# Expert layer: gate and up sums of the two-block items taken with the weights standing still and 192 rows moving

## The reference, cut to what matters

```
def expert_block(args):
    tok, e = args
    xb = u[tok]
    gu = xb @ w_gu[e] + b_gu[e]
    gate = jnp.minimum(gu[:, :D_FF], SWIGLU_LIMIT)
    up = jnp.clip(gu[:, D_FF:], -SWIGLU_LIMIT, SWIGLU_LIMIT)
    act = (up + 1) * gate * jax.nn.sigmoid(SWIGLU_ALPHA * gate)
    return act @ w_down[e] + b_down[e]
```

## Time and profile before

| | |
|---|---|
| median of 3 runs | 2235.86 us (2235.25 to 2238.87) |
| the profiled execution: its own time | 2238.45 us |
| the profiled execution: span in the trace | 2236.4 us |
| instructions in it | 34316 |
| PE busy | 2161.3 us, 97% of the span |
| DVE busy | 1698.4 us, 76% |
| ACT busy | 1364.3 us, 61% |
| DMA | 548.15 MB, 245 GB/s in the mean |
| granted TensorE clock | 0.98 of full speed in the mean |

### The profile page before, as it was taken

The page is one execution under the profiler, slowest core; times in us unless marked ns, Lnnn a source line. Parts: engine busy times, 40 slices in busy tenths (PEclk is TensorE's granted clock), DMA queues, the critical chain, the costliest instruction groups (busy, mean ns, idle before and its releaser), DMA issues. The chain is left out here.

```text
span 2236.4 us, 34316 instructions
## 1 busy us (share of the span) xinstructions
PE 2161.3 (97%) x10582; PEld 1773.3 (79%) x10583; DVE 1698.4 (76%) x2091; ACT 1364.3 (61%) x1632; POOL 396.6 (18%) x436
## 2 busy tenths in 40 slices
PE   7999999979959999999999999999999999999997
PEld 7987777757848888888888888888888888888884
DVE  5426667776667668879979978679996669997897
ACT  4324665543446556757757756568775557776775
POOL 0000000003331221312212212212220122221121
PEclk9999999989969999999999999999999999999997
DMA  4111101227868667969969969669996669998897
GB/s 163 41 47 34 57 34 43 100 64 208 211 206 294 233 227 281 365 244 367 371 242 367 368 240 332 239 239 383 373 380 242 218 235 334 392 364 316 295 366 288
DMA packets 106509, 548.15 MB, mean 245 GB/s; under 512 B 17911, under 2 KB 28664, under 8 KB 51546
## 3 DMA queue, kind: packets, MB, share of 16 engines
q1 hardware_dynamic: 87850, 504.63, 60.7%
q0 software_dynamic: 18608, 42.85, 8.0%
HBM read 516.18 MB, written 41.47 MB: 249 GB/s over the span
## 5 line engine op out<-in xcount | busy, mean ns | idle before, releaser
L2343 DVE TENSOR_TENSOR wl<-raw,wh 128x2048 fp32r<-128x2048 f32 x423 | 958.5, 2285 | 43.1 <-PE sums L2165 26.8
L2227 ACT ACTIVATE wh<-raw 128x2048 fp32r<-128x2048 f32 x425 | 806.0, 1915 | 92.5 <-DMA raw<-in_w_experts 50.2
L2149 PE MATMUL sums<-wh,xh 128*128 128x512 f32 x1120 | 438.0, 391 | 0.0
L2148 PE MATMUL sums<-wl,xh 128*128 128x512 f32 x1120 | 438.0, 391 | 0.0
L2147 PE MATMUL sums<-wh,xl 128*128 128x512 f32 x1120 | 437.3, 390 | 0.0
L2082 POOL DMA_INDIRECT h_dram<-y,pairs_mine x47 | 121.4, 2584 | 808.9 <-DVE y L2396 485.0
L2148 PEld LDWEIGHTS sums<-wl,xh 128*128 128x128 f32 x1120 | 210.8, 188 | 45.1
L2149 PEld LDWEIGHTS sums<-wh,xh 128*128 128x128 f32 x1120 | 210.8, 188 | 44.7
L2147 PEld LDWEIGHTS sums<-wh,xl 128*128 128x128 f32 x1120 | 211.2, 189 | 43.1
L2147 PE MATMUL sums<-wh,al 128*128 128x512 f32 x560 | 230.2, 411 | 0.6 <-DVE al L2387 0.2
L2149 PE MATMUL sums<-wh,ah 128*128 128x512 f32 x560 | 219.4, 392 | 0.0
(11 more groups left out here) (370 smaller groups left out, 3596.4 us busy)
## 6 DMA issues: line engine op xcount, KB each, us to landing
raw<-in_w_experts SPq DMA_DIRECT2D x426, 1024.0 KB
raw<-in_w_chan SPq DMA_DIRECT2D x20, 512.0 KB, 3.3
o_gate<-in_x SPq DMA_DIRECT2D x8, 512.0 KB, 5.5
raw<-in_w_out SPq DMA_DIRECT2D x8, 512.0 KB, 5.4
ht<-in_x SPq DMA_DIRECT2D x8, 512.0 KB, 8.1
h_dram<-ht SPq DMA_DIRECT2D x8, 512.0 KB
u_dram<-ut SPq DMA_DIRECT2D x8, 512.0 KB
h_all<-h_dram SPq DMA_DIRECT2D x8, 512.0 KB, 7.0
```

The lines of the kernel that those rows point to most:

```text
L2148: pe.matmul(out, hi[:, n, :], w_lo[:, kk, :], start=False, stop=False)
L2149: last = pe.matmul(out, hi[:, n, :], w_hi[:, kk, :], start=False, stop=half == 1 and kk == 3)
L2227: nc.scalar.activation(wh[ch % HIGHS][:, :, :], raw[ch % RAW][:, :, :], ACT.Copy).then_inc(h_split.sem, 1)
L2343: dve.tensor_tensor(wl[ch % LOWS][:, :, :], raw[ch % RAW][:, :, :], wh[ch % HIGHS][:, :, :], ALU.subtract).then_inc(l_split.sem, 1)
```

## The change

Two-block items alone compute the gate and up sums in another way. The weights stand still, in pieces of 128 inputs by 128 features, and all 192 tokens move. A new tile xx holds for each slice of inputs high x of the 192 rows and the rest of x of the 192 rows. For each of the 4 slices and 4 pieces of 128 features in a chunk (`by_weights`) one matmul moves 384 rows (high w by high x and rest of x) and one moves 192 (rest of w by high x). The sums have features on the partitions, so nothing is transposed for the down products, and there are no bias matmuls: ACT copies the 192 sums of rest of x (`copy_low`), DVE adds them and the bias, which is now a column (`fold`, own_bias), and clamps (`clamp_tiles`). Three pairs of PSUM banks (`ring`) take the sums in turn, and PE waits in `tile_free` and `begin_sums` until a pair is read. The second block's rows are transposed, and split by `high_second` and `low_second`, in two halves of 4 slices; chunk 0 waits for the first half, chunk 1 for the second. One chunk's `high` and one chunk's `low` move from the end of an item to the start of the next. `out` uses tile tg in place of hh. One table more (b_columns, 256 KB) and a table cut in two are loaded ahead of the expert layer. One-block items keep their products.

```diff
 HALF_ROWS = P // 2
+ROWS = P + HALF_ROWS
...
+            sp.dma_start(k.b_columns[:, :, :], k.d["b_columns"]).then_inc(small_loaded.sem, 16)
+            sp.dma_start(k.pick_cons[:, :], k.d["pick_consts"]).then_inc(small_loaded.sem, 16)
...
+        xx = sb("xx", [P, KT, 2, 2 * P], F32R)
+        xh, xl = xx[:, :, 0, 0:P], xx[:, :, 1, 0:P]
         ah, al = sb("ah", [P, KT, P], F32R), sb("al", [P, KT, P], F32R)
-
-        xb = sb("xb", [P, KT, P], F32R)
         ab = sb("ab", [P, KT, P], F32R)
-        sel = sb("sel", [P, 2, P], F32R)
-
-        tg = sb("tg", [P, 2, 256])
-        uc = sb("uc", [P, 2, 256])
-        hh = sb("hh", [H, 512])
-        av = [sb(f"av{s}", [P, 2, 256]) for s in range(2)]
+        sel = sb("sel", [P, P], F32R)
+        own_bias = sb("own_bias", [P, 4 * 4])
...
+        a_ps = ps("a_ps", [P, 2, 512])
+
+
+        ring = [k.sums[:, 0:2, :], k.sums[:, 2:4, :], a_ps[:, :, :]]
...
+            def begin_sums(i, g, blocks):
                 if g < 2:
                     pe.wait_ge(y_read.sem, y_read.at(i, g - 1))
+                elif blocks == 2 and g == 4:
+                    pe.wait_ge(gate_ready.sem, gate_ready.at(i, 4))
                 else:
                     pe.wait_ge(gu_read.sem, gu_read.at(i, g - 1))
 
-                for b in range(blocks if g < 4 else 0):
-                    pe.matmul(acc[g % 2][b][:, :], sel[:, b, :], bias[:, g * 512:(g + 1) * 512], start=True, stop=False)
+                if g < 4:
+                    pe.matmul(acc[g % 2][0][:, :], sel[:, :], bias[:, g * 512:(g + 1) * 512], start=True, stop=False)
+
+            def tile_free(i, g, j):
+
+                if g == 0:
+                    pe.wait_ge(y_read.sem, y_read.at(i, j // 2 - 1))
+                elif (g, j // 2) in ((1, 1), (2, 1), (3, 1)):
+                    pe.wait_ge(gate_ready.sem, gate_ready.at(i, g))
+                elif g > 1:
+                    pe.wait_ge(gu_read.sem, gu_read.at(i, g - 1))
+
+            def by_weights(i, ch):
+
+                g, half = GROUP_OF[ch], HALF_OF[ch]
+                pe.wait_ge(*low_done(i, ch))
+                w_hi, w_lo = wh[ch % HIGHS], wl[ch % LOWS]
+                for j in range(4):
+                    if half == 0 and j % 2 == 0:
+                        tile_free(i, g, j)
+                    out = ring[(2 * g + j // 2) % len(ring)][:, j % 2, :]
+                    own = slice(j * P, (j + 1) * P)
+                    for kk in range(4):
+                        n = half * 4 + kk
+                        pe.matmul(out[:, 0:2 * ROWS].rearrange("p (a b) -> p a b", b=ROWS), w_hi[:, kk, own], xx[:, n, :, 0:ROWS],
+                                  start=n == 0, stop=False)
+                        last = pe.matmul(out[:, 0:ROWS], w_lo[:, kk, own], xx[:, n, 0, 0:ROWS], start=False, stop=n == KT - 1)
+                    if half == 1 and j == 1:
+                        last.then_inc(gates_made.sem, 1)
+                last.then_inc(parts_used.sem, 1)
...
                 if blocks == 2:
                     pe.wait_ge(xg_loaded[1].sem, xg_loaded[1].at(i, 16))
-                    turn(1)
+                    for half in range(2):
+                        turn(1, range(4 * half, 4 * half + 4))
+                    for ch in range(8):
+                        if ch < 2:
+                            pe.wait_ge(x_low.sem, x_low.at(i, ch + 1))
+                        by_weights(i, ch)
                 else:
-                    pe.sem_inc(x_turned.sem, 1)
-                pe.wait_ge(sel_ready.sem, sel_ready.at(i, 1))
-                if blocks == 2:
-
-                    biases(i, 0, blocks)
-                    for ch in range(2):
-                        first_block(i, ch)
-                    pe.wait_ge(x_low.sem, x_low.at(i, 1))
-                    for ch in range(2):
-                        second_block(ch).then_inc(parts_used.sem, 1)
-                for ch in range(2 if blocks == 2 else 0, 8):
-                    products(i, ch, blocks)
-                    if ch >= 3 and ch % 2 == 1:
-                        turn_act(i, (ch - 3) // 2, blocks)
+                    pe.sem_inc(x_turned.sem, 2)
+                    pe.sem_inc(gates_made.sem, gates_made.per)
+                    pe.wait_ge(sel_ready.sem, sel_ready.at(i, 1))
+                    for ch in range(8):
+                        products(i, ch, blocks)
+                        if ch >= 3 and ch % 2 == 1:
+                            turn_act(i, (ch - 3) // 2)
...
+            def high_second(i, half):
+                act.wait_ge(x_turned.sem, x_turned.at(i, half + 1))
+                at = slice(4 * half, 4 * half + 4)
+                nc.scalar.activation(xx[:, at, 0, P:ROWS], x_ps[:, at, 0:H], ACT.Copy).then_inc(x_high.sem, 1)
+
+            def copy_low(i, g, part):
+
+                if g == 0 and part == 0:
                     act.wait_ge(y_read.sem, y_read.at(i, 0))
+                if part == 0:
+                    act.wait_ge(gates_made.sem, gates_made.at(i, g + 1))
+                    to = tg[:, 0:2 * ROWS].rearrange("p (a b) -> p a b", b=ROWS)
                 else:
-                    act.wait_ge(gate_ready.sem, gate_ready.at(i, g))
-                    act.wait_ge(up_ready.sem, up_ready.at(i, g))
-                nc.scalar.activation(hh[:, :], acc[g % 2][1][H:, :], ACT.Copy).then_inc(folded.sem, 1)
+                    act.wait_ge(parts_used.sem, parts_used.at(i, LAST_CHUNK[g] + 1))
+                    to = uc[:, 0:2 * ROWS].rearrange("p (a b) -> p a b", b=ROWS)
+                sums = ring[(2 * g + part) % len(ring)][:, :, ROWS:2 * ROWS]
+                nc.scalar.activation(to, sums, ACT.Copy).then_inc(low_copied.sem, 1)
...
             def item(i, blocks):
                 if blocks == 2:
-                    high_second(i)
+                    high_second(i, 0)
+                    high_second(i, 1)
+                high(i, HIGHS - 2)
                 high(i, HIGHS - 1)
                 for g in range(4):
                     high(i, 2 * g + HIGHS)
                     if blocks == 2:
-                        fold_high(i, g)
+                        copy_low(i, g, 0)
+                        copy_low(i, g, 1)
                     silu(i, g, blocks)
...
                 high(i, CH + 3)
                 out(i, 0, blocks)
                 out(i, 1, blocks)
-                high(i, CH + 4)
                 if blocks == 1:
                     act.wait_ge(y_read.sem, y_read.at(i, 2))
-                    act.sem_inc(folded.sem, folded.per)
+                    act.sem_inc(low_copied.sem, low_copied.per)
...
+            def low_second(i, half):
+                dve.wait_ge(x_high.sem, x_high.at(i, half + 1))
+                at = slice(4 * half, 4 * half + 4)
+                dve.tensor_tensor(xx[:, at, 1, P:ROWS], x_ps[:, at, 0:H], xx[:, at, 0, P:ROWS], ALU.subtract).then_inc(x_low.sem, 1)
...
+            def fold(g, j, part):
+
+                sums = ring[(2 * g + j // 2) % len(ring)][:, j % 2, 0:ROWS]
+                return dve.scalar_tensor_tensor(out=part, in0=sums, scalar=own_bias[:, 4 * g + j:4 * g + j + 1],
+                                                in1=part, op0=ALU.add, op1=ALU.add)
+
+            def clamp_tiles(i, g):
+                dve.wait_ge(low_copied.sem, low_copied.at(i, 2 * g + 1))
+                for j in range(2):
+                    last = fold(g, j, tg[:, j * ROWS:(j + 1) * ROWS])
+                last.then_inc(second_ready.sem, 1)
+                dve.wait_ge(second_ready.sem, second_ready.at(i, 2 * g + 1))
+                t = tg[:, 0:2 * ROWS]
+                dve.tensor_scalar(t, t, LIMIT, None, ALU.min).then_inc(gate_ready.sem, 1)
+                dve.wait_ge(low_copied.sem, low_copied.at(i, 2 * g + 2))
+                for j in range(2):
+                    last = fold(g, 2 + j, uc[:, j * ROWS:(j + 1) * ROWS])
+                last.then_inc(gu_read.sem, 1)
+                dve.wait_ge(gu_read.sem, gu_read.at(i, g + 1))
+                t = uc[:, 0:2 * ROWS]
+                dve.tensor_scalar(t, t, LIMIT, -LIMIT, ALU.min, ALU.max).then_inc(second_ready.sem, 1)
+                dve.wait_ge(second_ready.sem, second_ready.at(i, 2 * g + 2))
...
             def item(i, blocks):
                 if blocks == 2:
-                    low_second(i)
+                    low_second(i, 0)
+                    low_second(i, 1)
+                    dve.wait_ge(sel_ready.sem, sel_ready.at(i, 1))
+                low(i, 2)
                 low(i, 3)
...
                 if blocks == 2:
                     out_second(i, 0)
-                low(i, CH + 2)
-                if blocks == 2:
                     out_second(i, 1)
```

More of the change, by code:

```diff
@@ L2110, in _, with turn @@
             pe.sem_inc(parts_used.sem, parts_used.credit)
-            def turn(b):
-                for n in range(KT):
+            def turn(b, tiles):
+                for n in tiles:
                     last = pe.transpose(x_ps[:, n, :], xg[b][:, n * P:(n + 1) * P], k.c["ident"])
```

(36 more changed lines are left out.)

165 lines of the change are left out of this document (78 added, 87 removed).

## The result

| | median | runs | ratio to before (95% interval) |
|---|---|---|---|
| before | 2238.87 us | 2235.25 to 2244.16, 7 runs | |
| changed | 2249.16 us | 2243.05 to 2251.99, 7 runs | 1.0041 (1.0023 to 1.0059) |

A forecast was written before the change was run, and what follows sets the result against it. PE was taken to bound two-block items, with no stall to remove. Terms -45.4 - 0.9 + 28.2 + 7 + 1 = -10.1 us took the 2235.86 us median to 2226 us, 0.4% faster; range over all 2206 to 2250, forecast's own 2216 to 2235.

The forecast's parts named there:

- Removed: Two-block items: 8 bias matmuls and 16 transposes of activations go, 3.78 us an item, 45.4 us in all.
- products: Two-block items: 128 pairs at 0.2828 us replace 160 products, 36.20 for 36.27 us an item, 0.9 us gained in all.
- The bias alone: Two-block items: the 8 bias matmuls removed, 8 x 0.2267 = 1.81 us an item.
- the floor: Pairs: the 192-row matmul costs the next tile's load, 0.1106 us, not 0.0905; rival without it 2195 us, chance 0.06.
- Start waits: Start of two-block items: PE waits for the split rows, 7 x 2.1 + 5 x 2.7 = 28.2 us added.
- The clock: Two-block starts: full clock forecast; rival had it fall in new gaps, 2.4 us each, 2245 with 8, chance 0.14.
- Moved chunk: One-block items after two-block items: DVE's `low` of chunk 2 delays the first turned activations, 1.0 us times 7, 7 us.
- Costed at nothing: Two-block items: ACT's `copy_low`, DVE's `fold` and clamps fit in free time, no wait at chunk 8; 0 us.
- Setup: Ahead of the expert layer: two more loads (272 KB) before a wait DVE already has, +1 us, between 0 and 2.

The follow-up runs named there:

- kernel without split: The changed kernel with the second block's rows left at zero: ACT and DVE don't split them, PE doesn't wait for them; 2204.38 us, ratio 0.9855.
- first kernel with chunk 0 apart: The changed kernel with chunk 0 in two passes: high weights by first block's rows, then, behind the wait, pairs of 128 and 192 rows; 2223.56 us, ratio 0.9939.
- `low` back: The changed kernel with DVE's rest of chunk 2 back at the end of the item, ACT's order as in the changed kernel; 2248.62 us, ratio 1.0045.

## Why the prediction was wrong

The sum was -10.1 us; the spans of the profiled executions differ by +8.2. Term by term:

**Removed and products: right in sum, in part by luck.** -46.3 us was forecast for both. The kernel without split has 56.35 us for 60.17, 12 x -3.82 = -45.8. The bias alone, 21.8 us, is settled by the run without it. But the 128 pairs of an item of the kernel without the split take 36.47 us (from 1099.15 to 1135.62) where 36.20 was forecast and 36.27 stood before: the products cost 2.4 us more in all 12 items, not 0.9 less. Then what was removed gave 48.2 us for the 45.4 forecast. Two errors of some 3 us cancel, and that is luck. Of the pair, 0.2828 us forecast and 0.285 measured, the sum came within 1% and its parts didn't: the distances are 198 and 88 ns, not 172 and 111. What the load adds shows behind the long matmul. The prediction took 264 rows for its nearest price; the trace before also has 576 matmuls of 256 rows (L129 to L131, acc), 0.118 us apart, on the same line. Three runs support the floor: the pair didn't shrink with the short matmul's rows, it did with the long one's, and two short ones together take 224 ns, twice 112. So the 10% fewer rows bring nothing. That it is the load which sets this floor is the reading that fits all three; no run changed the load. The Trainium skill (TensorE: Matmul & The Clock Gate, section "LDWEIGHTS (loading the stationary operand)") has P / 1.2 ns for such a load, 107 ns for 128 columns; the 112 ns of the second pass are 5% above it. Its rule for the spacing (same page, section "Back-to-back issue gap"), N / 2.4 + 2.5 ns, gives 0.245 us for the pair and isn't met here; the section calls it the gap of an isolated matmul and says that it under-counts at small N, which the prediction left out.

**Start waits: right.** Forecast 7 x 2.1 + 5 x 2.7 = 28.2 us; PE's row of waits has 28.4, in 12 waits. In the items it is 31.3: 58.69 - 56.35 = 2.34 and 59.34 - 56.35 = 2.99 us, in items at full clock. The row counts less because its idle time begins when the last transpose has gone its way through the array (1.03 us into the item), while without the wait the first pair starts at 0.79 us (1099.15 - 1098.36). The copies, the loop's branches and their order came as in the earlier trace rows.

**The clock: the step that failed.** The forecast had the clock at full through all starts, so the fall stands in its sum at nothing; as a rival it had a chance of 0.14. The ground was that the layer before stood at full clock, and the prediction says itself that this layer had no gap like the new ones, so it was no evidence on gaps. 8 of 12 starts fell. The rival's time with 8 falls, 2245, is near the measured one, but its price of a fall was too high, 2.4 us for the 1.5 to 1.6 of each. The 12 items are 721.4 - 12 x 56.35 - 31.3 = 13.9 us longer than their work and waits. 12.5 of it are the falls, more than the whole gain forecast. The other 1.4 are in two items (at 686.87 and 808.67) in which the pairs stand 0.290 us apart from end to end, where in the other ten they stand 0.2845 apart. The same step of 0.6 us an item is in four items of the first kernel with chunk 0 apart, at full clock, so it isn't the fall; its cause is open. The filler, which adds work in PE's idle time and changes nothing else, gives 15 us back in the items of the trace (1558.7 to 1543.7), 13.8 of them in the two-block items, and turns slower into slightly faster.

**Moved chunk: mechanism only half right.** 7 us forecast, 11.5 measured (261.4 for 249.8 us in the 7 items). Forecast was a delay of the first turned activations. Against the same matmuls before, the first turn is 0.16 to 0.19 us late in each of the 7 items, 1.2 us in all; 8.3 us come at the turns 18 to 25 us into the item and 2.0 behind them. That loss in the middle comes through the DMAs. The first 10.56 us of the same item, before and changed:

```profile
1491.21:1501.77 10.56, 10.56 (x48) 8.77 (x47) 8.21 (x8) 9.14 (x7) 5.95 (x4) 1.00 0.95 291
```

```profile
1494.44:1505.00 10.56, 10.56 (x48) 8.71 (x47) 7.93 (x6) 7.04 (x6) 6.44 (x4) 1.00 0.48 106
```

The DMA share falls from 0.95 to 0.48, since SP loads a raw buffer only when `low` has read it. All 7 items show it: 0.93 to 0.97 before, 0.48 to 0.51 changed, and 0.75 to 0.79 with `low` back, where SP's first load of the item is issued 0.2 us into it and not 5.8. 22 us into the item the chunk that is missing shows:

```profile
1516.97 1.91 ACT L2266 ACTIVATE wh<-raw 128x2048 fp32r<-128x2048 f32 x1 [2.49 <-DMA raw<-in_w_experts]
...
1518.79 0.40 ACT L2302 ACTIVATE tg<-tg 128x256 f32<-128x256 f32 x1
...
1519.28 0.42 DVE L2447 SCALAR_TENSOR_TENSOR av<-uc,tg 128x256 f32<-128x256 f32 x1 [1.47 <-issue]
...
1519.76 0.44 PE L2139 MATMUL a_ps<-cons,av 128*128 128x128 f32 x2 [1.72 <-DVE av L2447]
```

ACT waits 2.5 us for the chunk (1.2 us for the same one before); the activation behind it in ACT's order is late, so DVE's product, so PE's turn. That moving `low` alone undoes the loss is shown by the three kernels that do it; that it goes through this wait of ACT is read from the traces, in which ACT waits longer for chunks in all 7 items than in the same ones before.

**Costed at nothing: right.** No wait stands at chunk 8. Setup, the other one-block items and the end together measured -2.7 us where +1 was forecast (-1.7, from 577.6 to 575.9 us, in the one-block items; 0.3 ahead of the layer; -1.3 behind it, 38.4 to 37.1 us). The forecast's +1 for the setup can't be told: the layer starts between 648.5 and 653.9 us in the traces of this study.

Sum: -45.8 + 31.3 + 13.9 + 11.5 - 2.7 = +8.2, the difference of the spans. The terms are worked out from that difference's parts, so it must close; what the runs tell apart are the start waits and the falls (no split, filler), the bias and the moved chunk.

Left open is why the same wait of 2.1 us ends in a fall at four starts after a one-block item and not at the other three, and what sets the two spacings of the pairs.

## What to carry to other kernels

A wait put into a gapless TensorE stretch costs itself and what the clock then takes; price both, and don't read "the clock stood at full" as evidence where there was no gap. Work that needs nothing new, even dearer work, belongs into the gap: the split first chunk turned +0.4% into -0.6%. When fewer rows move per standing tile, check that each matmul still outlasts the load of the next tile, and when a chunk's reader is moved, follow the buffer to the DMA that waits for it.

## What the hardware showed that was not expected

A fall of the clock doesn't hit the wait but the work behind it: in the 8 items PE became slow between 0 and 1.5 us after its restart (at 690.06 with the first matmul, at 1379.5 after ten), and stayed so for some 3.4 us in the item shown. And in pairs of a long and a short matmul the spacing behind the short one follows its own rows (88 ns for 192, 60 for 128), while what its load costs appears behind the long one (198 and 228 ns for the same 384 rows): only the pair's sum can be read.
